# Output projections and the second feed-forward layer by seven products of block sums instead of eight

## The reference

```
x = x + MIXED @ W_OUT                                   # mixed: two gated attention outputs
h = rmsnorm(x, ln_mlp_g)
x = x + square(relu(h @ w_mlp_up)) @ W_MLP_DOWN         # 1024 -> 4096 -> 1024
x = x + (fox_attention(...) * silu(gate)) @ W_OUT_A     # causal, with decay
x = x + (swa_sink_attention(...) * silu(gate)) @ W_OUT_B   # sliding window of 128, 16 query heads
```

## Time and profile before

| | |
|---|---|
| time, median of 3 | 1772.15 us (1770.3 to 1772.17) |
| profiled execution | 1769.92 us, span 1768.1 us, granted clock 0.966 |
| busy: PE, DVE, ACT, POOL | 95%, 53%, 41%, 22% of the span |
| chain that ended last | PE 67%, DVE 11%, issue 10%, ACT 9%, POOL 3% |
| matmuls of line 2010, 128x512 | 4416 of the 9314 |

### The profile page before, as it was taken

The page is one execution under the profiler, slowest core; times in us unless marked ns, Lnnn a source line. Parts: engine busy times, 40 slices in busy tenths (PEclk is TensorE's granted clock), DMA queues, the critical chain, the costliest instruction groups (busy, mean ns, idle before and its releaser), DMA issues.

```text
span 1768.1 us, 24731 instructions
## 1 busy us (share of the span) xinstructions
PE 1678.7 (95%) x9314; PEld 1318.8 (75%) x9314; DVE 933.9 (53%) x1675; ACT 726.6 (41%) x1643; POOL 383.9 (22%) x517
## 2 busy tenths in 40 slices
PE   7999998998879998999999999999999989997989
PEld 6887667887755555888888888888887767885757
DVE  3785674356346666344443244234836774457772
ACT  4324553143336665224332133133325553434550
POOL 5451332023125663011000000000113330022330
PEclk9999998999959999999999999999999998998979
DMA  7222002423012222322322333223230004230111
GB/s 187 96 78 90 25 25 83 143 93 122 1 42 58 62 59 67 126 102 83 95 97 99 101 101 104 96 77 138 96 97 25 26 25 143 96 95 2 49 49 48
DMA packets 107205, 141.38 MB, mean 80 GB/s; under 512 B 30348, under 2 KB 55204, under 8 KB 106848
## 3 DMA queue, kind: packets, MB, share of 16 engines
q1 hardware_dynamic: 106032, 139.10, 24.6%
q0 software_dynamic: 992, 0.86, 0.5%
q10 hardware_dynamic: 80, 0.02, 0.0%
HBM read 125.24 MB, written 4.24 MB: 73 GB/s over the span
## 4 chain that ended last, share of the span: by engine, by line
PE 67%; DVE 11%; issue 10%; ACT 9%; POOL 3%; DMA 0%; ACTq 0%; SPq 0%; POOLq 0%; DVEq 0%
PE ps L2010 50%; PE ps L2462 3%; PE ps L2245 2%; PE ps L2266 2%; ACT pbd L948 2%; DVE spl L1163 2%; DVE nm L1491 2%; PE ps L2281 1%; PE ps L2419 1%; ACT pb L892 1%; DVE qkt L1509 1%; PE ps L2443 1%; ACT qkt L969 1%; PE ps L2351 1%; ACT pts L956 1%
## 5 line engine op out<-in xcount | busy, mean ns | idle before, releaser
L2010 PE MATMUL ps<-spl,ht 128*128 128x512 f32 x2496 | 578.4, 393 | 10.3 <-DVE xk L1696 5.9
L2010 PEld LDWEIGHTS ps<-spl,ht 128*128 128x128 f32 x2496 | 472.7, 190 | 110.1 <-DVE xk L1696 6.3
L1186 DVE TENSOR_TENSOR spl<-raw,spl 128x1024 fp32r<-128x1024 f32 x168 | 222.1, 1364 | 396.3 <-ACT spl L721 396.3
L721 ACT ACTIVATE spl<-raw 128x1024 fp32r<-128x1024 f32 x168 | 168.5, 1052 | 463.5 <-PE ps L2010 437.2
L2010 PE MATMUL ps<-ht,spl 128*128 128x512 f32 x960 | 220.4, 391 | 2.0 <-DVE spl L1186 2.0
L2010 PEld LDWEIGHTS ps<-ht,spl 128*128 128x128 f32 x960 | 181.2, 189 | 40.5 <-issue 2.9
L2010 PE MATMUL ps<-spl,uu 128*128 128x512 f32 x768 | 174.7, 389 | 0.0
L2010 PEld LDWEIGHTS ps<-spl,uu 128*128 128x128 f32 x768 | 144.1, 188 | 29.8
L2462 PE MATMUL ps<-ht,spl 128*128 128x512 f32 x576 | 155.2, 408 | 2.7 <-DVE mx L1546 2.6
L1872 POOL TENSOR_TENSOR sq<-qkv 128x2048 f32<-128x2048 f32 (+1 forms) x15 | 51.5, 3434 | 326.0 <-ACT qkv L764 311.4
L2462 PEld LDWEIGHTS ps<-ht,spl 128*128 128x128 f32 x576 | 102.7, 190 | 23.8 <-DVE mx L1546 4.8
(11 more groups left out here) (311 smaller groups left out, 2223.5 us busy)
## 6 DMA issues: line engine op xcount, KB each, us to landing
raw<-w_in SPq DMA_DIRECT2D x30, 1024.0 KB, 5.1
raw<-w_mlp_up SPq DMA_DIRECT2D x16, 1024.0 KB, 5.3
raw<-w_mlp_down SPq DMA_DIRECT2D x16, 1024.0 KB, 5.0
raw<-w_in_a SPq DMA_DIRECT2D x16, 1024.0 KB, 5.4
raw<-w_in_b SPq DMA_DIRECT2D x8, 1024.0 KB, 5.5
raw<-w_proj_diff SPq DMA_DIRECT2D x4, 1024.0 KB, 6.8
...
```

Source lines behind the costliest of these rows:

```text
L721: act.activation(SPL[:, n % 2, HI, 2 * k:2 * k + 2], RAW[:, n % 2, 2 * k:2 * k + 2], ACT.Copy).then_inc(hi_done, 4)
L1186: dve.tensor_tensor(SPL[:, n % 2, LO, 2 * k:2 * k + 2], RAW[:, n % 2, 2 * k:2 * k + 2], SPL[:, n % 2, HI, 2 * k:2 * k + 2].bitcast(F32), A ...
L2010: last = pe.matmul(PS[:, b0 + b], left[:, x], right[:, y], start=(kt == 0 and i == 0), stop=(kt == UK * g["units"] - 1 and i == 2))
```

## The change

The product of a 512x1024 operand and a 1024x1024 weight is cut into 2x2 blocks on both sides. Instead of eight block products there are seven, of sums of blocks (Winograd's form of Strassen's scheme). A pair of groups (`pair`) now has five and two units. Each is a product of 256 tokens by 512 rows by 512 columns: 2 tiles x 4 steps x 3 = 24 matmuls (`one_of_seven`).

- Left side: four sums of blocks. VectorE makes s0 and s1 (`sums`), GpSimd s2 and s3; ScalarE and VectorE split each (`sum_high`, `sum_low`).
- Weights: the second 512 columns go to a new buffer `RX`; GpSimd makes four sums of 128x2048 in place in `RX` and `RAW` (`combine`). All seven are split as units.
- Result: products are added to quarters of `X` by VectorE, nine additions of 128x1024 (`adds`); two PSUM pairs accumulate across products, so TensorE waits for the addition (`acc`) before products 2, 4 and 6.
- The feed-forward goes in quarters: two first-layer groups, then a pair. The norm's scale is spread to a row (`spread_row("mlp")`) and multiplied in before the square, by VectorE out of PSUM; ScalarE squares.
- `RX` for `w_out_a` and `w_out_b` is loaded only after the last scores. The parked residual comes back behind it in two halves.
- The last sliding queries' norm moves into `attend_beside`: step one behind the first turns, step two behind the first maxima and gates.

```diff
+HALF = S // 2
+SEVEN = (("a", 0, 0), ("a", 0, 1), ("s", 1), ("a", 1, 1), ("s", 2), ("s", 0), ("s", 3))
+SUM_ORDER = (1, 0, 2, 3)
+LAST_TILES = (2, 3, 0, 1)
+def pair(name, weight, row, src):
+    return [(name + "0", weight, 0, row, len(SEVEN) - 2, "seven", src, ("residual", 0)),
+            (name + "1", weight, W, row, 2, "seven", src, ("residual", 1))]
...
-    runs["merge"] += [(f"wo{i}", "w_out", W * i, 0, 2, "tok", "ht", ("residual", i)) for i in range(2)]
-    half = FF // 2
+    runs["merge"] += pair("wo", "w_out", 0, "ht")
+    part = FF // 4
     runs["mlp"] = sum([
-        [(f"up{h}{i}", "w_mlp_up", half * h + W * i, 0, 2, "col", "ht", ("relu2", i)) for i in range(4)]
-        + [(f"dn{h}{i}", "w_mlp_down", W * i, half * h, 4, "tok", "uu", ("residual", i)) for i in range(2)]
-        for h in range(2)], [])
+        [(f"up{h}{i}", "w_mlp_up", part * h + W * i, 0, 2, "col", "ht", ("relu2", i)) for i in range(2)]
+        + pair(f"dn{h}", "w_mlp_down", part * h, "uu") for h in range(4)], [])
...
+                    x, y = RAW[:, r % 2], RAW[:, (r + 1) % 2]
+                    free[r], free[r + 1], free["x", p] = last.get(r % 2), last.get((r + 1) % 2), last_x
+                    for i, src in enumerate((x, y, x, y, RX[:, 0], x, RX[:, 1])):
+                        at[n + i] = src
+                    for i in range(2):
+                        ready[n + i] = (raw_full[(r + i) % 2], 16 * ((r + i) // 2 + 1))
+                    for i, k in ((2, 2), (3, 3), (4, 1), (5, 4)):
+                        ready[n + i] = (combined, 4 * p + k)
+                    ready[n + 6] = (rx_full[1], 16 * p + 16)
+                    last[r % 2], last[(r + 1) % 2], last_x = n + 5, n + 3, n + 6
...
+        def bank_pair(g, i):
+            b = 4 * (g["group"] % 2 if g["begin"] else 1 - g["group"] % 2)
+            k = (b, b + 2, b, 4 - b, b, 6 - b, 4 - b)[i]
+            return PS[:, k:k + 2]
...
+                    if c:
+                        if g["weight"] == "w_out":
+                            sp.wait_ge(freed["dve"], RUNS["merge"][1]["freed"])
+                        for a, weight in ((FOX, "w_out_a_2"), (SWA, "w_out_b_2")):
+                            if g["weight"] == weight:
+                                sp.wait_ge(*need(a, "s", 8 * a.units))
+                        sp.dma_start(RX[:, u], src).then_inc(rx_full[u], 16)
...
+                        act.wait_ge(*((u_relu, 3 * g["relus"] + b + 1) if b < 3 else (freed["dve"], g["freed"])))
+                        act.activation(square[:, b], R2[:, b], ACT.Square).then_inc(u_sq, 1)
...
+            def sum_high(g, i):
+                p, k = g["pair"], SUM_ORDER[i]
+                act.wait_ge(*((sums_a, 2 * p + 2) if i < 2 else (sums_b, 3 * p + (1 if i == 2 else 3))))
+                act.activation(SPLIT_SUMS[g["src"]][:, k, HI], SUMS[g["src"]][:, k, LO], ACT.Copy).then_inc(sum_hi, 1)
...
+                    dve.wait_ge(*row_kept("mlp"))
+                    dve.wait_ge(unit_used, g["unit"] + g["units"])
                     for b in range(4):
-                        if b < 3:
-                            dve.wait_ge(u_relu, 3 * g["relus"] + b + 1)
-                        else:
-                            dve.wait_ge(freed["act"], g["freed"])
-                        dve.tensor_tensor(R2[:, b], R2[:, b], R2[:, b], ALU.mult).then_inc(u_sq, 1)
+                        dve.scalar_tensor_tensor(R2[:, b], PS[:, b0 + b], 0.0, RB["mlp"], ALU.max, ALU.mult)\
+                           .then_inc(u_relu if b < 3 else freed["dve"], 1)
...
+            def sums(g):
+                p, to = g["pair"], SUMS[g["src"]]
+                dve.wait_ge(unit_used, g["unit"])
+                dve.tensor_tensor(to[:, 0, LO], source(g, 1, 0), source(g, 1, 1), ALU.add).then_inc(sums_a, 1)
+                dve.wait_ge(sums_a, 2 * p + 1)
+                dve.tensor_tensor(to[:, 1, LO], to[:, 0, LO], source(g, 0, 0), ALU.subtract).then_inc(sums_a, 1)
+                sum_low(g, 0)
+            def sum_low(g, i):
+                k = SUM_ORDER[i]
+                dve.wait_ge(sum_hi, 4 * g["pair"] + i + 1)
+                dve.tensor_tensor(SPLIT_SUMS[g["src"]][:, k, LO], SUMS[g["src"]][:, k, LO],
+                                  SPLIT_SUMS[g["src"]][:, k, HI].bitcast(F32), ALU.subtract).then_inc(sum_lo, 1)
+            def adds(g, u, norm):
+                p, n = g["pair"], g["first"]
+                def add(i, j, k):
+                    x = quarter(i, j)
+                    return dve.tensor_tensor(x, bank_pair(g, k), x, ALU.add)
+                if not g["begin"]:
+                    if u == 0:
+                        dve.wait_ge(unit_used, n + 6)
+                        dve.wait_ge(freed["dve"], g["freed"] - 1)
+                        if norm:
+                            for t in range(2):
+                                x = X[:, 2 + t, W:D]
+                                dve.tensor_tensor(x, bank_pair(g, 5)[:, t], x, ALU.add).then_inc(x_res, 1)
+                        else:
+                            add(1, 1, 5)
+                        dve.wait_ge(acc, 6 * p + 3)
+                        add(0, 1, 5).then_inc(acc, 1)
+                    elif not norm:
+                        dve.wait_ge(unit_used, n + 7)
+                        dve.wait_ge(acc, 6 * p + 6)
+                        add(0, 1, 6).then_inc(freed["dve"], 1)
+                    return
+                dve.wait_ge(unit_used, n + u + 1)
+                if u == 0:
                     if g["weight"] == "w_out":
                         dve.wait_ge(x_in[0], 32)
                     if g["weight"] == "w_out_a_2":
+                        dve.wait_ge(x_back[0], 16)
+                    add(0, 0, 0).then_inc(acc, 1)
+                elif u == 1:
+                    dve.wait_ge(acc, 6 * p + 1)
+                    add(0, 0, 1).then_inc(acc, 1)
+                elif u == 2:
+                    add(0, 1, 2).then_inc(acc, 1)
+                elif u == 3:
+                    if g["weight"] == "w_out_a_2":
+                        dve.wait_ge(x_back[1], 16)
+                    add(1, 0, 3).then_inc(acc, 1)
+                else:
+                    dve.wait_ge(acc, 6 * p + 4)
+                    add(1, 0, 4).then_inc(acc, 1)
+                    add(1, 1, 4).then_inc(freed["dve"], 1)
...
+                    if g["begin"]:
+                        sums(g)
                     for u in range(g["units"]):
                         ahead = 0 < norm < TAIL and k == len(groups) - 1 and u == g["units"] - 2
+                        if g["kind"] == "seven":
+                            adds(g, u, norm if k >= len(groups) - 2 else 0)
                         if ahead:
                             for kt in range(NT):
                                 low_x(norm, kt)
                         if g["unit"] + u + 2 < end:
                             split_lo(g["unit"] + u + 2)
+                        if g["begin"] and u < 3:
+                            sum_low(g, u + 1)
...
+                if a.is_swa:
+                    norm_one(RUNS["swa_in"][-1])
...
+                if a.is_swa:
+                    norm_two(RUNS["swa_in"][-1])
...
+            def combine(g):
+                p, n, r = g["pair"], g["unit"], g["raw"]
+                x, y = RAW[:, r % 2], RAW[:, (r + 1) % 2]
+                for i in range(2):
+                    pool.wait_ge(rx_full[i], 16 * p + 16)
+                pool.tensor_tensor(RX[:, 0], RX[:, 1], RX[:, 0], ALU.subtract).then_inc(combined, 1)
+                pool.wait_ge(lo_done, 2 * n + 2)
+                pool.wait_ge(combined, 4 * p + 1)
+                pool.tensor_tensor(x, RX[:, 0], x, ALU.add).then_inc(combined, 1)
+                pool.wait_ge(lo_done, 2 * n + 4)
+                pool.wait_ge(combined, 4 * p + 2)
+                pool.tensor_tensor(y, y, x, ALU.subtract).then_inc(combined, 1)
+                pool.wait_ge(sums_a, 2 * p + 2)
+                to, two = SUMS[g["src"]], SPLIT_SUMS[g["src"]]
+                pool.tensor_tensor(to[:, 2, LO], source(g, 0, 0), source(g, 1, 0), ALU.subtract).then_inc(sums_b, 1)
+                pool.wait_ge(lo_done, 2 * n + 6)
+                pool.tensor_tensor(x, RX[:, 1], x, ALU.subtract).then_inc(combined, 1)
+                pool.wait_ge(sum_lo, 4 * p + 1)
+                pool.wait_ge(sums_b, 3 * p + 1)
+                pool.tensor_tensor(to[:, 3, LO], source(g, 0, 1), two[:, 1, HI].bitcast(F32), ALU.subtract)\
+                    .then_inc(sums_b, 1)
+                pool.wait_ge(sums_b, 3 * p + 2)
+                pool.tensor_tensor(to[:, 3, LO], to[:, 3, LO], two[:, 1, LO].bitcast(F32), ALU.subtract)\
+                    .then_inc(sums_b, 1)
...
+            def one_of_seven(g, i, n, by_tile):
+                operand, p, bank = SEVEN[i], g["pair"], bank_pair(g, i)
+                if operand[0] == "s":
+                    pe.wait_ge(sum_lo, 4 * p + 1 + SUM_ORDER.index(operand[1]))
+                if i in (2, 4, 6):
```

(30 more changed lines are left out.)

244 lines of the change are left out of this document (143 added, 101 removed).

## The result

The changed kernel takes 1864.08 us (median of 4, 1862.01 to 1866.72), the kernel before 1771.22 beside it (1769.99 to 1772.17): 1.0518 times as long, 95% interval 1.0505 to 1.0530. The forecast was 1817, with a range of 1778 to 1840. The side was right, the size half of what came: +47 forecast, +93 measured.

A forecast was written before the change was run, and what follows sets the result against it. TensorE was taken to bound the kernel. Feed-forward +21, w_out +16, w_out_a +5, w_out_b +6, smaller parts +1.5 and the norm -3 gave +47 on 1769.92, so 1817 us; range 1778 to 1840.

The forecast's parts named there:

- What bounds the kernel, and what the matmuls are worth: Whole kernel: TensorE sets the end; removing 168 matmuls at 0.2267 us gains 38.1 us, 5.44 a pair.
- the signs that the forecast named: Profile after: 5.44 us products, gaps before products 1 to 3, w_out gap of 10 or more, TensorE busy some 38 less.
- The hidden layer's chain: Start of a feed-forward pair: the hidden layer's first low part makes product 1 2.7 us late.
- The sum of the gaps: Feed-forward pair: products 1 to 4 late by 2.7, 4.2, 3.0 and 0.9 us, 10.8 in all; +5.3 a pair.
- Its sum for w_out: w_out: products late by about 4, 12.6, 3.0 and 0.8 us; 59.4 against 43.5, +16.
- That for w_out_a: w_out_a: product 2 late by 6.4 us, products 3 and 4 by 3.0 and 0.8; 48.7 in all, +5.
- a rival at +20: Stalls inside a pair bring TensorE's clock down once a pair, seven times 2.8 us, giving 1837; chance 0.10.
- The shared price: Where two-tensor SBUF operations of VectorE and GpSimd meet, VectorE runs at 0.38 of its speed, GpSimd at 0.72.
- The early weight sum: w_out_a: first weight sum starts 4 us before product 0, GpSimd busy until 9, product 2 6.4 us late.
- Rival (a): Engines do not meet, VectorE's parts keep 1.18 us beside GpSimd; sum -4.5, 1765 us; chance 0.10.
- The norm: Sliding queries: VectorE fills its wait for GpSimd, first normaliser comes near 1603.5; -3 us (0 to -9).
- the dense rates: Where the engines meet, VectorE at 0.22 and GpSimd at 0.81 of speed; +63, 1833 us; chance 0.13.

The follow-up runs named there:

- the stall run: Kernel before, with extra VectorE additions ahead of the low parts of eight feed-forward units so that TensorE waits; 1820.3 us against 1770.4.

## Why the prediction was right and wrong

- **What bounds the kernel, and what the matmuls are worth.** Right. Undisturbed products start 5.44 apart, and 168 matmuls are gone. But of the signs that the forecast named, TensorE's busy time down by some 38 us did not come (1680.2 for 1678.7), and that leads to the failed step below.
- **The hidden layer's chain.** Right to 0.1 us: 2.58 against 2.7 where nothing meets.
- **The sum of the gaps.** The feed-forward stage stands still for 42.5 us in all, 10.6 a pair; forecast 10.8. That is luck in its parts. In the pair shown product 1 was later (5.17 for 2.7: GpSimd's second sum held the split ahead of the hidden layer, 4.10 for 2.36, and its third the first low part, 3.35 for 2.50), products 2 and 3 earlier (2.86 and 0.8 for 4.2 and 3.0), product 4 later (2.64 for 0.9); in the other pairs product 1 was late by 4.0 to 5.3. w_out stood still for 24 us (3.8 and 2.4 in product 1, 15.1 before product 2, 2.6 before product 4), forecast 20.4. Over the whole program TensorE is idle for 93 us more, where the forecast had 85. (Its sum for w_out is off by 0.9: 38.1 and 20.4 are 58.5, not 59.4. That for w_out_a is off by 0.4, and that for w_out_b has no terms.)
- **The failed step: the clock.** The sum had it at nothing and a rival at +20 with a chance of 0.10, as a thing that might happen beside the forecast. But the forecast itself set four gaps of 1 to 4 us into each pair, and the stall run shows that each of 3 us costs 1.7 more. It was a term of the sum, not a rival: 38.6 us (some 33 without the last matmuls' way), of the 47 that the forecast was short. By stage: 22.5 in the feed-forward (353.5 us busy; 351.7 before, less 21.8, plus 1, is 331), 5.4 in w_out (45.3 busy; 45.3 before, less 5.4), 3.7 in w_out_a's stage and 7.4 in w_out_b's. The earlier trace rows had shown it: 2.8 lost behind thin work, which I used for one fall a pair where there are two or three. Each cost 1.7 to 2.5 (products of 7.2 to 8.1 us for 5.6); not every gap did, for behind 1.94 and 1.90 the product took 5.69.
- **The shared price.** Wrong in kind. 0.38 and 0.72 were averages over two rows; the traces show a lock for the length of GpSimd's instruction, so a VectorE operation of any size pays up to 4.6 to 5.5 us. It could be read in the earlier trace rows already: two halves that take 2.36 alone took 5.76 beside one operation of 4.45. GpSimd's own prices were short too: 4.6 to 5.5 for 3.60 to 4.45, and 3.3 to 3.4 for 1.9 in the two sums that make the fourth block sum. The price of 3.60 was taken from a square of one tensor, and a weight sum reads two.
- **A place that was overlooked.** The early weight sum was counted as a gain for w_out_a (product 2 only 6.4 late) and not as a load on the attention's last steps: +8.3 there, and 4.3 in the sliding one. The queue that it was moved past was VectorE's, through the lock.
- **Rival (a)**, the engines not meeting, was made real and gives about 1775, not 1765 (1778.7, less 4 for what lies ahead of w_out): its -4.5 lacked 14 us of clock and had the gaps too wide by 5 to 6.
- **The norm.** -3 forecast (0 to -9), -5 measured.
- **The range** ended at 1840. It left out the dense rates together with the clock. Adding these (1833 + 20) and the attention's end (8) gives 1861, near what came, but that would be luck. The dense rates held in w_out alone (24 us idle, where they give 25.4); the feed-forward stood still as the forecast had it; and the clock was 38.6, not 20.

What stays open: how the 85 us that hang on GpSimd's sums divide between their dates and the lock. The run without them removes both, and no run has the dates without the lock. Nor do the runs divide the clock: 14.5 us of it are there without GpSimd's sums, so some 24 of the 38.6 came with the gaps that these make.
